# Delta scan: fillers cut to halves of 256 tokens, a fifth half ahead of each read of the state

## The reference, cut to what matters

```python
proj = h @ in_w                       # (1024 x 1024) @ (1024 x 4112)
def step(state, inp):                 # once per chunk, one after the other
    w_c, u_c, attn_c, q_c, k_c, e_c = inp
    v_new = u_c - einsum('bhcd,bhde->bhce', w_c, state)
    o_c = einsum('bhcd,bhde->bhce', q_c, state) + einsum('bhcm,bhme->bhce', attn_c, v_new)
    state = state * e_c[..., None, None] + einsum('bhcd,bhce->bhde', k_c, v_new)
    return state, o_c
```

## Time and profile before

| | |
|---|---|
| time, median of 3 runs | 2165.67 us (2165.45 to 2166.63) |
| profiled execution: its own time | 2162.22 us |
| profiled execution: its span | 2160.5 us |
| mean granted TensorE clock | 0.993 |
| TensorE busy | 2081.9 us (96%) |
| VectorE busy | 1360.8 us (63%) |
| ScalarE busy | 643.2 us (30%) |
| GpSimd busy | 216.1 us (10%) |

### The profile page before, as it was taken

The page is one execution under the profiler, slowest core; times in us unless marked ns, Lnnn a source line. Parts: engine busy times, 40 slices in busy tenths (PEclk is TensorE's granted clock), DMA queues, the critical chain, the costliest instruction groups (busy, mean ns, idle before and its releaser), DMA issues. The chain is left out here.

```text
span 2160.5 us, 20801 instructions
## 1 busy us (share of the span) xinstructions
PE 2081.9 (96%) x6930; PEld 1065.1 (49%) x6930; DVE 1360.8 (63%) x1918; ACT 643.2 (30%) x1063; POOL 216.1 (10%) x180
## 2 busy tenths in 40 slices
PE   6999999999999999999899999999999999999998
PEld 5444444445556555556555445554444444444443
DVE  5787743364755746746742487528999997634633
ACT  4345521333433443434311521012321111241021
POOL 0000001112212212112000000001000000003200
PEclk8999999999999999999999999999999999999999
DMA  9333389321111111111320317269722222334021
GB/s 340 119 112 122 105 278 204 113 66 35 46 32 34 46 29 36 38 37 36 139 40 1 107 59 120 59 185 253 179 59 78 66 71 73 102 103 136 20 98 58
DMA packets 243824, 207.17 MB, mean 96 GB/s; under 512 B 52204, under 2 KB 202785, under 8 KB 243745
## 3 DMA queue, kind: packets, MB, share of 16 engines
q1 hardware_dynamic: 213393, 157.25, 24.5%
q0 software_dynamic: 13056, 42.99, 8.1%
q10 hardware_dynamic: 17312, 6.10, 1.3%
HBM read 182.55 MB, written 60.33 MB: 112 GB/s over the span
## 5 line engine op out<-in xcount | busy, mean ns | idle before, releaser
L2295 PE MATMUL bank<-hT,ring 128*128 128x512 f32 x576 | 254.2, 592 | 0.0
L2295 PE MATMUL bank<-resid,ring 128*128 128x512 f32 x432 | 191.3, 592 | 0.0
L2295 PEld LDWEIGHTS bank<-hT,ring 128*128 128x128 f32 x576 | 109.4, 190 | 137.8 <-issue 136.6
L1279 PE MATMUL bank<-hT,ring 128*128 128x512 f32 x336 | 157.7, 595 | 1.8 <-ACT silu_z L1515 1.8
L3205 DVE SCALAR_TENSOR_TENSOR yT<-s_arena,yT 128x1024 f32<-128x1024 f32 x120 | 153.0, 1275 | 0.0
L3205 DVE SCALAR_TENSOR_TENSOR s_arena<-s_arena 128x1024 f32<-128x1024 f32 x112 | 142.8, 1275 | 0.0
L2267 PE MATMUL bank<-hT,ring 128*128 128x512 f32 x320 | 139.4, 594 | 0.0
L2295 PEld LDWEIGHTS bank<-resid,ring 128*128 128x128 f32 x432 | 82.1, 190 | 103.3 <-issue 102.6
L1869 DVE SCALAR_TENSOR_TENSOR memory<-memory,col_exp_last,bank 128x128 f32<-128x128 f32 x64 | 22.2, 347 | 153.9 <-PE bank L1459 153.9
L2267 PEld LDWEIGHTS bank<-hT,ring 128*128 128x128 f32 x320 | 60.1, 190 | 73.7 <-issue 73.5
L2340 PE MATMUL bank<-ssm_y,ring 128*128 128x512 f32 x192 | 83.4, 592 | 0.0
(11 more groups left out here) (586 smaller groups left out, 3671.3 us busy)
## 6 DMA issues: line engine op xcount, KB each, us to landing
ada<-in_ada_w SPq DMA_DIRECT2D x8, 2048.0 KB, 8.1
ring<-in_gdn_in_w SPq DMA_DIRECT2D x32, 512.0 KB, 4.2
ring<-in_w_in SPq DMA_DIRECT2D x54, 256.0 KB, 2.9
ab_U_sums<-in_w_in POOLq DMA_DIRECT2D x6, 2048.0 KB, 19.9
resid<-in_x SPq DMA_DIRECT2D x8, 1024.0 KB, 8.9
ring<-in_lru_in_w SPq DMA_DIRECT2D x16, 512.0 KB, 3.9
ring<-ab_U_sums SPq DMA_DIRECT2D x32, 256.0 KB, 3.0
lru_arena<-in_ada_w SPq DMA_DIRECT2D x6, 1024.0 KB, 13.1
```

The costliest lines, as they stand in the source:

```text
L1279: last = nc.tensor.matmul(bank[:, to, :], w[:, k, :], v[:, k, :], start=(first and k == 0), stop=(k == KB - 1), skip_group_check=not only)
L2295: last = nc.tensor.matmul(bank[:, to, :], w[:, k, :], src[:, k, :], start=(start and k == 0), stop=(k == HK - 1), skip_group_check=not alone)
```

## The change

Behind `qk` 7 fillers are issued where there were 11. Within the scan of the first seven heads each matmul of 512 tokens is cut in two of 256 (the flag `by_halves`), each with a weight load of its own. A chunk gets five halves: two ahead of `new`, two ahead of `mem` and, as the new place, one behind `o`, that is ahead of the next chunk's `read`; in the last chunk this half comes directly ahead of what is behind the scan. Eight times five halves are 20 whole fillers where 16 were. All other places keep their numbers, and 4 whole fillers still stand behind the scan. In the last head the counts (the second numbers) are the same and nothing is cut.

```diff
+                    by_halves = [False]
...
                             for k in range(KB):
-                                last = nc.tensor.matmul(bank[:, to, :], w[:, k, :], v[:, k, :], start=(first and k == 0), stop=(k == KB - 1),
-                                                        skip_group_check=not only)
-                                if k == KB - 1:
-                                    px_pe.mark(last, name + pr)
-                                yield
+                                widths = (slice(0, HALF // 2), slice(HALF // 2, HALF)) if by_halves[0] else (slice(0, HALF),)
+                                for n, part_ in enumerate(widths):
+                                    last = nc.tensor.matmul(bank[:, to, part_], w[:, k, :], v[:, k, part_], start=(first and k == 0 and n == 0), stop=(k == KB - 1),
+                                                            skip_group_check=True if len(widths) > 1 else not only)
+                                    if k == KB - 1 and n == len(widths) - 1:
+                                        px_pe.mark(last, name + pr)
+                                    yield
...
                         each(R5, lambda c: kT[:, c, :], lambda c: qT[:, c, :], "qk")
-                        fill(11, 34)
+                        fill(7, 34)
...
                         for c in range(NCH):
                             if c == 0:
                                 fill(1, 0)
+                                by_halves[0] = True
...
                             nc.tensor.matmul(R5[:, 4, :], qT[:, c, :], memory[:, :], start=True, stop=True)
-                            fill(1, 2)
+                            fill(2, 2)
                             hd_dve.wait(pe, f"delta{c}", h)
                             hd_pe.mark(nc.tensor.matmul(R4[:, 4, :], invT[:, c, :], delta[:, 0, :], start=True, stop=True), f"new{c}")
-                            fill(1, 2)
+                            fill(2, 2)
...
                             hd_pe.mark(nc.tensor.matmul(R4[:, 4, :], attnT[:, c, :], delta[:, 1, :], start=True, stop=True), f"o{c}")
+                            fill(1, 0)
+                        by_halves[0] = False
                         fill(64, 2 * TT * KT)
```

## The result

Over 20 runs of each the median is 2167.6 us (2163.58 to 2172.65) against 2163.6 us (2159.32 to 2166.68) before: a ratio of 1.0022 with a 95% interval of 1.0015 to 1.0029. That is 4 us slower, clear of zero, and on the line of 0.2% that the prediction drew between "same" and "slower". The forecast of 2169.0 us was a rise of 3.3 us on 2165.67, the median of the three runs then known; the rise came out at 4.0, on a median that is 2.1 us lower with 20 runs.

What follows compares the result with a forecast made beforehand. The head was taken as a ring where `k_flip` and `v_flip` wait for VectorE and ScalarE. 0 + 0 + 1.3 (cut) + 0 + 2.0 (clock) = 3.3 us on 2165.67 gave 2169.0 us, range 2164.6 to 2176.0.

Steps and rivals of the forecast that it cites:

- line of 0.2%: Whole kernel: a difference under 0.2% (4.3 us) can't be told from no change.
- Where the head is bound: Loop head: a ring of three parts; only fillers taken off the part from `v_flip` to the scan's end gain time.
- The gap ahead of `Y16`: Behind `qk`: four fillers fewer come back as a wait of 3.0 to 3.2 us ahead of `Y16`; gain nothing.
- The rival by which the scan's gaps would give 21 us: Scan: gaps really free and fillers behind `qk` on the path, 2144.6 us; chance 0.06 for anything faster by over 0.2%.
- The fifth half: Ahead of `read` in the scan: 0.43 to 0.45 us, hidden in each chunk and covered in the tail; gain nothing.
- slack of 0.39 us: Scan: delaying `read` by 0.39 us costs TensorE nothing, since the query product waits for VectorE's `o`.
- The price of the cut: 16 scan fillers in seven heads: two halves cost 0.012 us more than a whole, 1.3 us in all (0 to 4.1).
- The late products: Products from `P1b` on, up to four fillers later: cost 0, or 2 us in all if chunk 2's copy is late.
- The clock: Around the gap at `Y16`: clock falls to 0.50, costing 0.5 us in four of seven heads, 2.0 us.
- slack behind `v_flip`: From `v_flip` to the next flips (`F16`), which wait for VectorE: 0.2 us of a late start is got back.
- Same or slower: Whole kernel: chance 0.62 for the same within 0.2%, 0.32 for slower, 0.06 for faster.
- rival of a dearer clock: At `Y16`: clock falls in every head, sometimes for two turns; 2177.5 us at 1.5 a head; chance 0.32 with milder cases.

Runs made afterwards that it cites:

- filled gap: Changed kernel plus four matmuls of 512 columns with unread results in the gap ahead of `Y16`, first seven heads; ratio 0.9999 to the kernel before.
- x_rounds: Changed kernel with 11 fillers behind `qk`, none ahead of `Y32`, `F32` and `Y64`, 3 behind the scan; ratio 0.9958 to the kernel before.
- x_whole: Kernel before, nothing cut, with 7 fillers behind `qk` and a whole filler ahead of `read` in every second chunk; ratio 1.0019 to the kernel before.
- x_cut: Kernel before with each head's 16 scan fillers cut in halves, no fifth half, all 11 fillers behind `qk`; ratio 1.001 to the kernel before.
- x_chunk: Changed kernel with one half per chunk moved from ahead of `new` to ahead of `read`; ratio 0.9923 to the kernel before.
- x_split: Changed kernel with 9 fillers behind `qk` in place of 7 and 2 behind the scan in place of 4; ratio 1.0005 to the kernel before.

## Why the prediction was right, step by step

- **Where the head is bound.** Right in what matters. A head is a ring in which `v_flip` and `k_flip` wait for VectorE and ScalarE, and fillers ahead of `v_flip` are worth nothing. The filled gap shows it from one side (24 us of added work cost nothing), `x_rounds` from the other (2.58 us of fillers a head taken off behind `v_flip` gave 1.12). One link reads otherwise than the prediction had it: it let `v_silu` wait for the value taps alone, which end at 663.47. ScalarE's own queue before the change is as follows:

```profile
660.32 1.90 ACTq L1561 DMA_DIRECT2D baseT<-x_scratch  x4
662.39 1.28 ACT L1563 ACT_TABLE_LOAD   x1 [8.36 <-issue]
```

The load of ScalarE's function table ends at 663.67, and `v_silu` starts 0.02 us later. In every head of the kernels before and after it starts 0.01 to 0.02 us behind this load, while its distance from the end of the taps goes from 0.19 to 0.44. So ScalarE's issues and its table load hold it at least as much as VectorE's taps do. Neither waits for a filler, so the forecast stands.
- **The gap ahead of `Y16`.** Right: 3.0 to 3.2 us were forecast, 3.02 to 3.09 are found and 3.36 in the first head. The rival by which the scan's gaps would give 21 us is out.
- **The fifth half.** Right in all its parts: `read` not late, the chunk not shorter, TensorE 0.43 us later behind the scan (4.31 in place of 3.88 from the last `mem` to the flip of the output), and the wait ahead of `k_flip` 0.18 in place of 0.61. The slack of 0.39 us was borne out by `x_whole`, where `read` comes 0.38 us later at no cost.
- **The price of the cut.** Mis-sized: 1.3 us were taken from the line through two shapes; it is 0.6. Here the Trainium skill's rule (TensorE: Matmul & The Clock Gate, section "Wait — 56ns, not 53.3ns?") was nearer, with 5 ns a pair as an estimate against 5.6 measured in `x_cut`. The line failed at its lower end: by the 512-column instructions and the price measured for those of 256, one of 128 columns would take 0.109 us, and it takes 0.112. Why is not shown.
- **The late products.** Costed at nothing, and nothing it is: the filled gap has them all as late as the changed kernel, and its heads are 84.2 us.
- **The clock.** The mechanism was right and the size low: four heads at 0.5 us were taken; it was five, at 0.3 to 0.6 us over the cut's price in four of them and 1.3 to 1.6 in the first (86.92 us against 85.28 to 85.62 in first heads without a fall), 2.9 to 3.3 us in all and not 2.0. Two parts offset in it. The slack behind `v_flip` can be twice what was assumed: where `v_flip` is 0.7 us late (30.84 in place of 30.14 behind `k_flip`), the way from there to the first `read` is 0.41 shorter (15.62 in place of 16.03), and only 0.3 remain. That holds for two of the four heads; where the fall came later, over `v_flip`, less of it was got back (head from 808.65: `v_flip` on time, 16.65 us to the first `read`). Against that, a fall for 6.8 us had been kept for the rival and came in one head.
- **Same or slower.** The forecast gave 0.62 to "within 0.2%" and 0.32 to slower. At 1.0022 with 1.0015 to 1.0029 the result sits on that bound; the clock's part took it there. The rival of a dearer clock was set apart from a mean of 0.45 us a head on, and 0.41 to 0.47 were found, so the rows do not part these two cases.
- **What was luck.** The rise of 3.3 us came near 4.0 with two terms off in opposite ways: 0.7 us too much for the cut, 0.9 to 1.3 too little for the clock. A few tenths more come from the spread of the first head, which was in no term.

Left open: which heads the fall hits. Behind gaps of 3.0 to 3.4 us it came in five of seven heads in the profiled execution (not in the second and sixth), in five of seven in `x_whole` (not in the third and seventh), in all seven in `x_chunk`, and in none behind the gaps of 1.3 to 1.7 us of `x_split`. Each kernel has one profile here. The mean clocks show more time at the lower clock in every run of the changed kernel, `x_whole` and `x_chunk` than in any run of the kernel before; whether the same heads fall in each was not measured.

## What to carry to other kernels

Before moving filler work, ask of the place that it comes from what the next instruction waits for: if that is another engine's chain, the filler was free, and taking it away buys only an idle stretch. Fillers are worth time only where they stand between a ready instruction and the chain that sets the end; here that was behind `v_flip` and ahead of `new`. And an idle stretch on TensorE isn't neutral: 3 us of it cost 0.3 to 0.6 us in most heads and 1.3 to 1.6 in one, while pieces of 1.4 and 1.0 us cost nothing.

## What the runs showed of the hardware beyond the forecast

- Work that nobody reads can pay: four extra matmuls in each of seven gaps (24 us of TensorE time) held the granted clock at 1.00 and took the changed kernel's 1.0022 back to 0.9999 (0.9987 to 1.0010).
- A float32 matmul cut from 512 columns to two of 256, each with its own weight load, costs 5.6 ns more in all at 2.4 GHz.
- Where the clock fell in a head of the changed kernel, it stayed at 0.50 for 3.4 us, once for 6.8. In the first head, all of `Y16` lay in the fall, and its eight matmuls of 128 columns took 3.57 us to the next start (496.98 to 500.55) in place of 1.79.
- The load of a function table on ScalarE ahead of `v_silu` took 1.28 us in every head of the kernels before and after.
